# Expanding cached keys: a third buffer of squares, score products behind the value products, low parts of six streams made by GpSimd

## What is computed

```python
def mla_expand(c_kv, w_kv_b, k_norm):
    kvb = (c_kv @ w_kv_b).reshape(b, S, MLA_HEADS, QK_NOPE + V_HEAD)
    k_nope = rmsnorm(kvb[..., :QK_NOPE], k_norm)      # 16 heads x 64
    return k_nope, kvb[..., QK_NOPE:]

def attend(q_nope, q_rope, k_nope, k_rope, v, q_pos, k_pos):
    s = (einsum('bqhd,bkhd->bhqk', q_nope, k_nope)
         + einsum('bqhr,bkr->bhqk', q_rope, k_rope)) * ATTN_SCALE
    s = where(mask, s, -inf)
    return einsum('bhqk,bkhd->bqhd', softmax(s), v)
```

## Time and profile before

| | |
|---|---|
| median of 3 runs | 1838.8 us (1838.54 to 1841.67) |
| the profiled execution's own time | 1838.99 us |
| its span | 1837.2 us |
| TensorE busy | 1809.3 us, 98% |
| VectorE busy | 1135.8 us, 62% |
| ScalarE busy | 827.9 us, 45% |
| GpSimd busy | 228.9 us, 12% |
| granted TensorE clock | 0.998 of full speed, mean |

### The profile page before, as it was taken

One profiled execution on the slowest core, in us unless ns is written; L12 is line 12 of the kernel. 1 busy time (PEld: TensorE's weight loads), 2 busy tenths in 40 slices (PEclk: granted clock), 3 DMA queues, 4 the chain that ended last, 5 costly groups with the idle time before them and its releaser, 6 DMA issues.

```text
span 1837.2 us, 28276 instructions
## 1 busy us (share of the span) xinstructions
PE 1809.3 (98%) x10567; PEld 1732.5 (94%) x10567; DVE 1135.8 (62%) x1706; ACT 827.9 (45%) x1420; POOL 228.9 (12%) x280
## 2 busy tenths in 40 slices
PE   9999999999999999999999999999998999999998
PEld 9999999799888999999999999996777999999998
DVE  6454447879889645444775454456778856454445
ACT  6333336665564433333553333346665544333333
POOL 1000110311311000011400001122112131000110
PEclk9999999999999999999999999999999999999999
DMA  6434444456352544454344434451124534444442
GB/s 212 135 117 136 139 138 153 153 207 235 122 206 87 193 125 127 124 149 138 115 143 118 135 116 140 139 170 40 47 85 142 166 116 127 133 120 131 143 137 76
DMA packets 68452, 249.48 MB, mean 136 GB/s; under 512 B 8264, under 2 KB 10568, under 8 KB 67088
## 3 DMA queue, kind: packets, MB, share of 16 engines
q1 hardware_dynamic: 58880, 206.86, 36.8%
q0 software_dynamic: 9488, 41.48, 6.6%
HBM read 235.51 MB, written 12.12 MB: 135 GB/s over the span
## 4 chain that ended last, share of the span: by engine, by line
PE 82%; DVE 10%; ACT 3%; DMA 2%; issue 2%; POOL 0%; SPq 0%; DVEq 0%; ACTq 0%; POOLq 0%
PE pair L1913 24%; PE pair L1914 24%; PE pair L1915 24%; DVE wlo L1245 2%; PE pair L2333 2%; PE pair L2335 2%; PE pair L2334 2%; DVE cy L1372 1%; DMA lowA<-in_cacheT 1%; DVE S L1468 1%; PE pair L2422 1%; PE pair L1920 0%; PE pair L1922 0%; PE pair L1921 0%; PE pair L2121 0%
## 5 line engine op out<-in xcount | busy, mean ns | idle before, releaser
L1913 PE MATMUL pair<-xh,whi 128*128 128x384 f32 x1960 | 660.3, 337 | 3.0 <-DVE xl L1255 2.0
L1915 PE MATMUL pair<-xh,wlo 128*128 128x384 f32 x1960 | 654.9, 334 | 0.0
L1914 PE MATMUL pair<-xl,whi 128*128 128x384 f32 x1960 | 654.8, 334 | 0.0
L1245 DVE TENSOR_TENSOR wlo<-raw,whi 128x1024 fp32r<-128x1024 f32 (+3 forms) x371 | 463.8, 1252 | 160.7 <-ACT whi L708 159.8
L708 ACT ACTIVATE whi<-raw 128x1024 fp32r<-128x1024 f32 (+2 forms) x369 | 378.0, 1028 | 261.9 <-PE pair L1915 257.8
L1913 PEld LDWEIGHTS pair<-xh,whi 128*128 128x128 f32 x1960 | 367.9, 188 | 10.0 <-DVE wlo L1245 3.9
L1914 PEld LDWEIGHTS pair<-xl,whi 128*128 128x128 f32 x1960 | 368.0, 188 | 1.6 <-issue 1.0
L1915 PEld LDWEIGHTS pair<-xh,wlo 128*128 128x128 f32 x1960 | 367.9, 188 | 0.0
L1265 DVE TENSOR_TENSOR tg<-pair,rstd 128x384 f32<-128x384 f32 x88 | 49.1, 558 | 326.2 <-PE pair L1915 325.5
L1913 PE MATMUL pair<-ah,whi 128*128 128x384 f32 x704 | 235.2, 334 | 0.0
L1914 PE MATMUL pair<-al,whi 128*128 128x384 f32 x704 | 235.1, 334 | 0.0
(11 more groups left out here) (408 smaller groups left out, 2202.2 us busy)
## 6 DMA issues: line engine op xcount, KB each, us to landing
raw<-in_stream SPq DMA_DIRECT2D x372, 512.0 KB, 3.6
S<-in_ssm POOLq DMA_DIRECT2D x4, 2048.0 KB, 9.3
out_ssm_s<-S POOLq DMA_DIRECT2D x4, 2048.0 KB, 7.8
seg<-acs_rows POOLq DMA_DIRECT2D x12, 512.0 KB, 6.0
cTb<-in_cacheT POOLq DMA_DIRECT2D x10, 512.0 KB, 4.3
kn<-rs_rows SPq DMA_DIRECT2D x16, 264.0 KB
lowC<-in_cache SPq DMA_DIRECT2D x8, 512.0 KB, 3.2
lowA<-in_cacheT POOLq DMA_DIRECT2D x6, 512.0 KB, 5.0
```

Of the source, the lines that this page charges most:

```text
L1245: V.tensor_tensor(wlo[:, r, 0:w], raw[:, r, 0:w], whi[:, r, 0:w].bitcast(F32), ALU.subtract).then_inc(lo_ready, 1)
L1913: M(out, whi[:, r, ws], mh_(k), start=first and k == k0, stop=False)
L1914: M(out, whi[:, r, ws], ml_(k), start=False, stop=False)
L1915: ins = M(out, wlo[:, r, ws], mh_(k), start=False, stop=last and k == k1 - 1)
```

## The change

Four things, all in the stage of the cached keys:

- `past_square` and `past_sums` use three buffers in `kn` instead of two; a square waits for the sum of w - 3.
- `p_scores` of the next heads stands behind the value products, ahead of expansions 8y + 6 and 8y + 7; iteration y makes the scores of heads 2y + 4 and 2y + 5, and those of 2 and 3 are made ahead of the first expansions.
- ACT's `past_split(y + 1)` stands ahead of `past_square(8y + 3)`, for y = 1 to 6, where it stood behind the high part of the head outputs.
- The low parts of streams 2 to 7 are made by GpSimd, each behind the load of its stream in POOL's queue; DVE keeps those of streams 0 and 1.

```diff
@@ gpsimd, loads of the latents
                 pool.dma_start(cTb[:, b % 2, :, 0:PAST], T["cacheT"][b]).then_inc(c_ld[b % 2], 16)
+                if b >= 2:
+                    pool.wait_ge(past_hi, b + 1)
+                    pool.wait_ge(past_lo, b)
+                    pool.tensor_tensor(cTl[:, b % 2, :, 0:PAST], cTb[:, b % 2, :, 0:PAST], cTh[:, b % 2, :, 0:PAST].bitcast(F32),
+                                       ALU.subtract).then_inc(past_lo, 1)
                 if b == 2:
                     pool.wait_ge(rs_ev, 1)
@@ scalar
             def past_square(w):
                 act.wait_ge(past_ps, w + 1)
-                if w < 2:
+                if w < 3:
                     act.wait_ge(key_turn_ps, 4)
                 else:
-                    act.wait_ge(past_sum, w - 1)
-                A(kn[:, w % 2, 0:512], bank[w % 2][:, :], ACT.Square).then_inc(past_sq, 1)
+                    act.wait_ge(past_sum, w - 2)
+                A(knf[:, 512 * (w % 3):512 * (w % 3) + 512], bank[w % 2][:, :], ACT.Square).then_inc(past_sq, 1)
...
+                if 2 <= y + 1 < STREAMS:
+                    past_split(y + 1)
                 past_square(8 * y + 3)
...
                 A(xh[:, y, 0:SEQ], bank[7 if y % 2 else 3][:, 0:SEQ], ACT.Copy).then_inc(oh_ready, 1)
-                if 2 <= y + 1 < STREAMS:
-                    past_split(y + 1)
                 past_square(8 * y + 6)
@@ vector
-                V.reduce_sum(ksq[:, st, b, 8 * g:8 * g + 8], kn[:, w % 2, 0:512].rearrange("p (h d) -> p h d", h=8),
+                V.reduce_sum(ksq[:, st, b, 8 * g:8 * g + 8], knf[:, 512 * (w % 3):512 * (w % 3) + 512].rearrange("p (h d) -> p h d", h=8),
                              axis=AX.X).then_inc(past_sum, 1)
...
-                        if 2 <= y + 1 < STREAMS:
-                            past_split(y + 1)
@@ tensor
             for y in range(MH // 2):
-                for x in (2 * y + 2, 2 * y + 3):
-                    if x < MH:
-                        p_scores(x)
+                if y == 0:
+                    p_scores(2)
+                    p_scores(3)
                 for i in range(4):
                     past_expand(8 * y + i)
...
+                for x in (2 * y + 4, 2 * y + 5):
+                    if x < MH:
+                        p_scores(x)
```

## The result

| | before | changed |
|---|---|---|
| median | 1838.52 us (9 runs, 1836.94 to 1841.67) | 1843.83 us (9 runs, 1842.95 to 1845.52) |
| ratio | | 1.0032, 95% interval 1.0023 to 1.0040 |
| profiled execution: own time / span | 1838.99 / 1837.2 us | 1843.27 / 1841.4 us |
| loop, first score product to first product behind the loop | 120.67 us | 126.13 us |
| attention of the running streams, from there to the first product of the head outputs | 89.38 us | 87.95 us |

The changed kernel is 0.32% slower. The loop grew by 5.5 us, almost the medians' difference of 5.3. The spans of the profiled executions differ by 4.2 only: the loop began 0.2 later, and the stage behind it was 1.4 us shorter in this one (more on that at the end).

What follows compares the result with a forecast made beforehand. It took TensorE, busy nearly all the time, as the bound. Terms +5.7 - 0.3 - 1.2 - 0.4 + 0.6 + 0.8 = +5.2 on 1838.99 us gave 1844.2 us, range 1841.5 to 1847.

Steps and rivals of the forecast that it cites:

- split ahead of square 8y + 3: ACT's order before expansion 8y + 5: 0.16 us of room, expansion 0.84 late plus 0.11 restart, 0.95 in iterations 1 to 6, +5.7.
- stream 4's load late: POOL's queue, iteration 3: the load behind the rotary query copies lands 0.4 to 0.8 us too late before square 27, +0.8.
- switch of operands: Scores behind value products: the late second matmul now falls between value and score products, may save up to 0.11 seven times, -0.3.
- wait at expansion 56: Start of iteration 7: GpSimd's earlier low part removes the wait, a start 1.08 us late plus 0.11 restart, -1.2.
- iteration 3's extra: Iteration 3 took 0.40 us more than iteration 1, from a late low part and squares held by late sums; -0.4.
- root and table load ahead of square 56: ACT, iteration 7: with expansion 56 earlier, expansion 58 waits 0.5 for square 56 and pays 0.11; +0.6 (0 to 0.9).
- third buffer: Squares' buffers: removes ACT's one wait of 1.3 us, at which TensorE did not wait; worth 0.
- GpSimd holds up DVE: Rival, chance 0.05: GpSimd's subtraction holds DVE's mask and maxima work 1.1 us an iteration, 6.4 on top, 1850.6 us.
- GpSimd's subtraction: Low parts of 1024 elements on GpSimd: taken as 2.7 us, by estimate 2.3; covered either way, so it costs 0.
- What the loop loses shows at the end in full.: Stage behind the loop: running streams' attention starts from the last sum of squares, so loop gains or losses show fully.
- the split fits in: Rival, chance 0.12: ACT finishes copies, split and square before TensorE asks; only gains remain, -1.9, 1837.1 us.
- about 5 us in all: Sign in the profile after: weight loads' waits for squares at expansions 8y + 5, six of some 0.8 us, where 2.5 stood.

## Why the prediction was right

It gave 1844.2 us, with 1841.5 to 1847; measured were 1843.8 (median) and 1843.3 (profiled). By its own terms, against the starts of TensorE's matmuls:

| term | predicted | measured |
|---|---|---|
| split ahead of square 8y + 3, six times 0.95 | +5.7 | +5.7, and 0.14 more in iteration 2 |
| stream 4's load late | +0.8 | +0.44 at expansion 29 |
| switch of operands | -0.3 | 0 |
| wait at expansion 56 | -1.2 | -1.2 |
| iteration 3's extra | -0.4 | -0.1 |
| root and table load ahead of square 56 | +0.6 | +0.5 |
| third buffer | 0 | 0 (shown alone) |
| sum | +5.2 | +5.5 |

- *The deciding term.* Argued from ACT's order and 0.16 us of room; right to the hundredth in four of six iterations. For the 0.14 of iteration 2 I have no cause: the split stands 0.90 us behind the copies there instead of 0.76, without a releaser in the trace, and does so with the low parts on DVE too. That nothing is given back was right as well.
- *Stream 4's load.* The place was right, the size half: expansion 29 starts 0.44 later than its like in iteration 1, and ACT waited 0.31 us for the load. For the other 0.13 no row shows a cause.

```profile
1326.80 1.06 ACT L1081 ACTIVATE cTh<-cTb 128x1024 fp32r<-128x1024 f32 x1 [0.31 <-DMA cTb<-in_cacheT]
```

- *The switch.* I had hoped that the late second matmul would fall away. It moved: from the value products it now lies inside the score products, 0.32 to 0.34 us between two starts.
- *Iteration 3.* I expected the whole 0.4 to go. Expansion 31 still starts 0.20 late, and pays 0.11. Here the rival "GpSimd holds up DVE", to which I gave 0.05, has its one foothold in the changed kernel: the scaling of the maxima took 2.14 us from 1328.21, and ACT then stood idle for 2.04.

```profile
1328.21 2.14 DVE L1775 TENSOR_SCALAR sm<-sm 128x2 f32<-128x2 f32 x1
...
1327.95 2.37 POOL L641 TENSOR_TENSOR cTl<-cTb,cTh 128x1024 fp32r<-128x1024 f32 x1 [4.58 <-ACT cTh L1081]
...
1330.39 0.40 ACT L1094 ACTIVATE Pb<-Pb,sm 128x128 f32<-128x128 f32 x1 [2.04 <-DVE sm L1775]
```

With the low parts on DVE, expansion 31 does not wait. The rival priced the hold on the mask addition, which is not held, and overlooked the scaling, which is. In the other iterations of the changed kernel the second head's scaling starts 2.26 us into the subtraction, 0.12 before its end, and takes 0.17: there is nothing left to hold, because the stall at expansion 8y + 5 has shifted DVE's work. Once that stall is mended, the hold is there in every iteration from 1 to 6: in the kernel with the split behind, 1.56 to 2.30 us six times.
- *GpSimd's subtraction.* I took 2.7 us from the nearest row; it measured 2.38. The estimate of 2.3 from the Trainium skill ("GPSIMD Engine Reference", section "Elementwise — side-by-side cycle accounting") was closer. Either was covered.
- *"What the loop loses shows at the end in full."* By the medians it does (5.3 against 5.5); in the profiled executions the stage behind gave 1.4 us back, see below. The rival "the split fits in" is excluded by the six waits.
- *The sum.* Its five misses, of 0.1 to 0.4 us, have both signs and come to 0.3. That +5.2 and +5.5 lie so close is luck in part; that the sum is made up of the one term of 5.7 is not.
- *The signs.* I had given "about 5 us in all" for the weight load's waits for squares; it was 9.5, of which the six are 7.2, since a weight load's wait begins 0.43 us before the matmul's. The matmuls' own waits for squares are 4.8 in all.

The expectation of the study that failed by most was that of the split behind its square, with the same step missing: I asked what ACT's move does to ACT and TensorE, and did not ask beside which instructions of DVE GpSimd would now run.

## What to carry to other kernels

An instruction that is moved ahead in a hand-written order delays what stands behind it, whether or not the engine is idle before the place: ask what the next instruction hands back, and how much room there is until it is asked for (here 0.16 us against 0.95). Here the early place that cost nothing by itself was the one just behind that hand-back. And once GpSimd takes over work of some length, look in DVE's timeline for instructions that are usually short and last until GpSimd's end, even on two numbers a partition, and give those to another engine or another moment.

## What the runs showed of the hardware

**A hold to the end of GpSimd's instruction.** A DVE `TENSOR_SCALAR` on 128x2 floats, SBUF to SBUF, lasts 0.17 us alone and up to 2.30 beside a GpSimd subtraction of two SBUF operands, ending within 0.03 us of it. All 16 in the kernel with the split behind (shortest, median and longest in ns), of which six were held, and the nine that were left in the kernel where seven were given to ACT:

```profile
L1775 DVE TENSOR_SCALAR sm<-sm x16: 169/170/2299, 1273.3 to 1372.4; 128x2 f32<-128x2 f32 x16
```

```profile
L1785 DVE TENSOR_SCALAR sm<-sm x9: 168/170/171, 1273.1 to 1367.1; 128x2 f32<-128x2 f32 x9
```

I had read the earlier trace rows as something for operations with two SBUF operands. The Trainium skill ("SBUF — State Buffer", section "SBUF: two separate sides") names DVE operations in a two-port mode as well, and says that whichever starts first has the shared ports for its whole instruction; the trace agrees, for one input and 2 elements. That this operation runs in such a mode no row shows.

It is not a matter of the size. In the kernel with the split back in its old place, GpSimd's subtractions fall beside other work of DVE, and there the `TENSOR_SCALAR` of 128x128 (L1785, 0.29 us alone) took 0.42 to 1.21 us six times, ending 0.08 to 0.09 behind GpSimd's, while the `RECIPROCAL` of 128x2 just before it took its usual 0.15:

```profile
1377.39 0.15 DVE L1784 RECIPROCAL sm<-sm 128x2 f32<-128x2 f32 x1
1377.58 1.21 DVE L1785 TENSOR_SCALAR Pb<-Pb,sm 128x128 f32<-128x128 f32 x1
...
1376.35 2.35 POOL L641 TENSOR_TENSOR cTl<-cTb,cTh 128x1024 fp32r<-128x1024 f32 x1 [11.80 <-ACT cTh L1081]
```

Reductions of DVE, and an addition with one operand in PSUM, were not held either.

**The clock after a wait.** A wait of 1.31 us of TensorE at the score products was followed by a granted clock of 0.53 over 3.6 us, that is, about the lower level of 1.2 GHz, with matmuls 0.43 us apart instead of 0.23. The lost half clock cost about 1.8 us in nine matmuls, more than the wait. But the wait's length alone does not decide. The changed kernel's six waits of 0.67 to 1.11 us left the clock at 1.00; so did four of 1.61 and one of 1.75 in the kernel with the split made twice, whose sixth, of 1.91, was followed by the half clock, and one of 1.74 at expansion 56 in the kernel with the split back. Behind expansions 21 and 29 of the kernel with the split made twice:

```profile
1315.10:1318.70 3.60, 3.60 (x25) 2.80 (x26) 2.58 (x7) 2.89 (x11) 1.93 (x1) 1.00 0.03 7
1331.39:1333.50 2.11, 2.11 (x5) 1.72 (x6) 2.04 (x6) 1.39 (x6) 1.91 (x1) 0.53 0.01 4
```

Nor, it seems, does it come each time: 3.6 us at 0.53 would lower an execution's mean granted clock by 0.0009, to 0.999, and five of the eleven executions of the kernel with the split behind show 1.000, though it is not shown that each had the wait of 1.31. What decides stays open.

**The stage behind the loop.** Over 13 profiled kernels the attention of the running streams took 87.7 to 88.4 us where the granted clock of the stretch 10 to 20 us behind the loop was 1.00 (five kernels, the changed one among them), and 89.0 to 89.9 where it was 0.83 or 0.66 (eight). Before, and then the changed kernel:

```profile
1398.20:1408.20 10.00, 6.87 (x42) 6.32 (x42) 9.11 (x19) 5.09 (x11) 1.78 (x3) 0.83 0.50 151
```

```profile
1403.90:1413.90 10.00, 6.44 (x48) 5.70 (x49) 9.58 (x20) 4.87 (x11) 1.78 (x3) 1.00 0.44 147
```

TensorE waits a third of this stretch in either. I don't know what decides which clock it gets: it follows neither the split's place nor where the low parts are made. Each kernel has one profile, and executions of one kernel differ too: over the eleven changed kernels with several, the 33 whose mean granted clock was 1.000 took 0.6 us less on average than their own kernel's median, and the 25 at 0.998 took 0.6 more. So single spans differ by about 1.3 us (the two groups' means) from what the loop alone would say, and the loop's length was taken as the measure. What decides stays open.
